# Order of the woven instruction programs written out for the first mixer and the second block's mixers, and chosen anew for the third block

## The chip, the cores and the metric

The kernel runs on one core of one Trainium2 chip. The metric is the device time of one execution in microseconds (us). The engines of the core take their own instruction streams and wait for one another through semaphores: TensorE (PE) multiplies matrices, VectorE (DVE) and ScalarE (ACT) do the elementwise work, GpSimd (POOL) issues gathers, SyncE (SP) issues nearly all other transfers. Everything is fp32; a large product is made of three fp32r products, each operand being split into a high and a low part.

## The reference, cut to what matters

Three transformer blocks follow one another on x (512 rows, 1024 columns).

```python
def first_block(x, c, ...):
    mod = silu(c) @ w_ada + b_ada               # 6 rows of 1024: shift, scale, gate twice
    h = rms_norm(x, norm1_w) * (1 + scale1) + shift1
    q, k, v, cb, cc, cx, iq, ik, iw = split(h @ w_in)
    # indexer: relu(iq . ik) weighted by iw over 8 heads, 128 keys kept for each query
    score = einsum(relu(einsum(iq, ik)), iw); sel = top_k(causal(score), 128)
    y_attn = softmax(rms_norm(q) . rms_norm(k)[sel]) @ v[sel]      # 8 heads of 64
    y_conv = cb * causal_conv3(cc * cx)
    x = x + gate1 * (concat(rms_norm(y_attn), rms_norm(y_conv)) @ w_out)
    return x + gate2 * peer_ffn(rms_norm(x) * (1 + scale2) + shift2, ...)

def second_block(x, ...):
    # band attention (8 heads), gated delta rule (4 heads, chunks of 64, after a conv of 4),
    # four causal window means (pool), three gated branch products, output product
    x = layer_norm(alpha * x + hybrid_mixer(x, ...))
    return layer_norm(alpha * x + hierarchical_moe(x, ...))

def third_block(x, ...):
    # four attentions (forgetting, block-sparse, stick-breaking, sliding window), gates, output product
    return x + concat(o_fox, o_moba, o_sb, o_swa) * silu(gates) @ w_out
```

## The kernel before, in words

The blocks run one after another, each as one or more stages. The first block is `first_mixer` (0 to 468 us of the span; names begin with firsts_) and the retrieval of `peer_ffn` (names peer_). The second is `mixers` (1822 to 2523), the routing and the experts (names slotted_). The third is `third_block` (3180 to 3622, names third_). Rows are kept in four tiles of 128, the contraction of 1024 in eight steps k.

Within `first_mixer`, `mixers` and `third_block` the work of one engine is given as several generator programs. Each yields before a part of its work; what it yields is a number, its estimated due time. `weave` (L1520) merges the programs of one engine: the one with the lowest number goes next. `weave_by` (L1536) merges them by a table instead: "b8 c6" means eight parts of the second program and six of the third. Before the change only the third block uses a table, `THIRD_ORDER`. The order decides in which sequence an engine's instructions stand in its queue; each engine takes its queue in that sequence, and waits where a semaphore isn't there yet.

The programs of `first_mixer`. `loads` (SP) brings c, the first third of w_ada (8 loads of 1 MB, firsts_ada_first), x, the constants; `weights_in` (SP) the pieces of w_in into three buffers firsts_raw; `ada_in` the rest of w_ada. `ada_tensor` multiplies silu(c) with the first four column blocks of w_ada (L649, 64 matmuls), `ada_vector` sums the other eight on DVE (L679, L682, 64 steps), each closed by a matmul L660. `rows_*` make h and its transpose hT (high and low). `rounded` (ACT L801) and `rests` (DVE L809) split a weight piece into high and low; `products` (PE L849) multiplies a piece: 8 steps k of 3 matmuls, 30 pieces, 720 matmuls. `rel_*` are the indexer's scores: PE L997, relu on ACT L1007, weighted sum on DVE L1019 and L1022, closed by L1026; then the picking, 16 rounds of MAX8 (L1033) and MATCH_REPLACE8 (L1038) on DVE. `soft_*` are 32 softmax works n (8 heads by 4 row tiles t, 128(t+1) keys): score L1078 on PE, bias L1119, maximum L1122 and its negation L1123 on DVE, exponential L1101 on ACT, transposes L1082 on PE, copy L1105 on ACT, mix with v L1088 on PE, copy L1126 on DVE (semaphore scaled). Work n uses bank n%2 of two. `closed_*` are the output product (L834 first half, L864 second half) and the second norm.

The programs of `mixers`: `products` (L1774, three matmuls a step k), `rounded` and `rests` (L1788, L1795), `band_*` (score L2050, transposes L2055, mix L2060), `pool_*` (window sums on DVE L1955 to L1958, matmul L1973), `conv_*` (L2252 to L2292), and `delta_*` in two streams for the gated delta rule: its PE steps L2329 to L2388, the norm of its output (square sums L2545, root ACT L2438, L2552, scaling L2555), transposes L2394 and the multiplication with the gate mixers_dg (L2566). The gate goes out to DRAM and comes back; ACT L1838 works on it once it has landed.

In the third block `stick_*` are the stick-breaking works (scores L3985, DVE L4037 to L4049, ACT L4021, PE L3991 and L3998).

## Time and profile before

| | before |
|---|---|
| median of three runs, us | 3620.53 (3618.37 to 3625.39) |
| profiled execution, us | 3623.54 |
| its span, us | 3621.8 |
| mean granted clock of PE, share of full | 0.931 |
| PE busy | 3155.4 us, 87% of the span |
| DVE busy | 2412.2 us, 67% |
| ACT busy | 1399.1 us, 39% |
| first mixer, us | 468 |
| mixers, us | 701 |
| third block, us | 442 |
| one split of a weight piece on DVE (L809), mean | 1.19 us |
| one ada step on DVE (L682), mean | 0.75 us |

In the rows further down a line is an instruction or a group of them: engine, source line, operation, output and inputs by their names, and in square brackets the time that the engine stood idle ahead of it and what ended that. PE matmuls overlap: the distance of two starts tells the rate, the duration doesn't. PEclk is the share of full clock that the throttle granted to PE (0.50 is 1.2 GHz, 1.00 is 2.4 GHz).

### The profile page before, as it was taken

Reading aid. Unit: us, or ns where it says so; the run is one execution under the profiler, and the core shown is the slowest. Engines: PE = TensorE matmul, PEld = TensorE weight load, DVE = VectorE, ACT = ScalarE, POOL = GpSimd, SP = SyncE. Lnnn points to the kernel's source line nnn. Section 1 sums busy time; section 2 is a strip of 40 time slices with the busy share of each in tenths; the row PEclk is TensorE's granted clock in tenths of the full one; section 3 lists DMA queues with packets and bytes.
Section 4 is the critical chain, followed back from the end, with each engine's and each line's share of the span. In section 5 each row is a group of like instructions: output and inputs, shape, how many; then the busy total and the mean of one; then the engine's idle time right before and its main releaser. Section 6 shows DMA issues by size and latency. Waiting matters only on the chain. (4 is left out here: it accounts for less than half of the span.)

```text
span 3621.8 us, 34663 instructions
## 1 busy us (share of the span) xinstructions
PE 3155.4 (87%) x11816; PEld 2012.9 (56%) x11816; DVE 2412.2 (67%) x4718; ACT 1399.1 (39%) x2337; POOL 717.6 (20%) x583
## 2 busy tenths in 40 slices
PE   8988889988787787777788999997599999949998
PEld 4655644433333333333366787776488888836666
DVE  4866446677767776777658445554688888845565
ACT  2323322222222222222243233342488888733564
POOL 0000024344444444444400000000122222100000
PEclk9988899998999899999899999998699999969999
DMA  8322169999999999999942222232799999831111
GB/s 283 111 82 87 47 244 393 404 400 422 421 408 421 417 414 421 413 414 413 416 116 58 65 73 70 68 111 76 257 354 374 377 371 372 317 107 48 53 41 65
DMA packets 351923, 905.62 MB, mean 250 GB/s; under 512 B 29953, under 2 KB 170753, under 8 KB 285570
## 3 DMA queue, kind: packets, MB, share of 16 engines
q0 software_dynamic: 84000, 549.52, 37.1%
q1 hardware_dynamic: 267746, 353.85, 29.0%
q8 instruction: 98, 1.61, 0.2%
q14 instruction: 79, 0.65, 0.1%
HBM read 896.45 MB, written 31.99 MB: 256 GB/s over the span
## 5 line engine op out<-in xcount | busy, mean ns | idle before, releaser
L258 PE MATMUL peer_acc<-peer_uv,peer_diag 128*128 128x512 f32 x2048 | 1004.1, 643 | 228.9 <-ACT peer_diag L314 223.2
L435 DVE CUSTOM_DVE_ANT_0 peer_uv<-peer_uv,firsts_h 128x1024 f32<-128x1024 f32 x512 | 627.3, 1226 | 345.9 <-DMA peer_uv<-in_peer_uv,peer_experts 344.6
L258 PEld LDWEIGHTS peer_acc<-peer_uv,peer_diag 128*128 128x128 f32 x2048 | 410.5, 205 | 803.6 <-issue 494.4
L210 POOL DMA_INDIRECT peer_uv<-in_peer_uv,peer_experts x512 | 593.4, 1159 | 1212.2 <-PE peer_acc L258 692.4
L3066 DVE TENSOR_TENSOR slotted_low<-slotted_raw,slotted_high 128x2048 fp32r<-128x2048 f32 x192 | 434.2, 2289 | 66.6 <-ACT slotted_high L3015 66.6
L3015 ACT ACTIVATE slotted_high<-slotted_raw 128x2048 fp32r<-128x2048 f32 x192 | 365.5, 1920 | 64.4 <-PE slotted_h L2972 51.8
L314 ACT ACTIVATE peer_diag<-all_consts,peer_weights 128x128 f32<-128x128 f32 x512 | 166.1, 391 | 325.6 <-DVE peer_weights L428 300.7
L305 ACT ACTIVATE peer_act_in<-peer_act_in 128x4 f32<-128x4 f32 (+1 forms) x130 | 26.6, 205 | 615.5 <-DVE peer_act_in L435 615.3
L2972 PE MATMUL slotted_h<-slotted_high,slotted_xT_high 128*128 128x512 f32 x512 | 205.2, 401 | 6.2 <-DVE slotted_low L3066 4.1
L2972 PE MATMUL slotted_h<-slotted_high,slotted_xT_low 128*128 128x512 f32 x512 | 201.8, 394 | 0.0
L2972 PE MATMUL slotted_h<-slotted_low,slotted_xT_high 128*128 128x512 f32 x512 | 201.7, 394 | 0.0
L1774 PE MATMUL mixers_acc<-mixers_xT_high,mixers_high 128*128 128x512 f32 x448 | 197.5, 441 | 1.7 <-DVE mixers_low L1795 1.7
L1774 PE MATMUL mixers_acc<-mixers_xT_high,mixers_low 128*128 128x512 f32 x448 | 179.7, 401 | 0.0
L1774 PE MATMUL mixers_acc<-mixers_xT_low,mixers_high 128*128 128x512 f32 x448 | 179.5, 401 | 0.0
L1795 DVE TENSOR_TENSOR mixers_low<-mixers_raw,mixers_high 128x1024 fp32r<-128x1024 f32 (+1 forms) x77 | 93.2, 1210 | 123.9 <-ACT mixers_high L1788 123.4
L2839 POOL MEMSET slotted_xg<- 128x4096 f32 x1 | 3.5, 3511 | 731.4 <-POOLq L60 731.4
L2934 POOL DMA_INDIRECT results<-slotted_ob,slotted_rows_out x32 | 32.3, 1008 | 461.7 <-ACT slotted_ob L3042 447.8
L2972 PEld LDWEIGHTS slotted_h<-slotted_high,slotted_xT_high 128*128 128x128 f32 x512 | 97.5, 190 | 27.3 <-DVE slotted_low L3066 4.3
L2972 PEld LDWEIGHTS slotted_h<-slotted_high,slotted_xT_low 128*128 128x128 f32 x512 | 97.4, 190 | 21.5
L3544 PE MATMUL third_acc<-third_hT_high,third_high 128*128 128x512 f32 x240 | 107.2, 447 | 1.5 <-DVE third_hT_low L3408 1.5
L2972 PEld LDWEIGHTS slotted_h<-slotted_low,slotted_xT_high 128*128 128x128 f32 x512 | 97.6, 191 | 19.2
L849 PE MATMUL firsts_acc<-firsts_hT_high,firsts_high 128*128 128x512 f32 (+1 forms) x240 | 104.7, 436 | 2.9 <-DVE firsts_low L809 2.9
(752 smaller groups left out, 5689.3 us busy)
## 6 DMA issues: line engine op xcount, KB each, us to landing
slotted_raw<-in_moe_w SPq DMA_DIRECT2D x192, 1024.0 KB, 8.1
mixers_raw<-in_w_in SPq DMA_DIRECT2D x56, 512.0 KB, 3.9
firsts_ada_raw<-in_w_ada SPq DMA_DIRECT2D x64, 256.0 KB, 2.8
third_raw<-in_w_in SPq DMA_DIRECT2D x30, 512.0 KB, 3.8
firsts_raw<-in_w_in SPq DMA_DIRECT2D x28, 512.0 KB, 4.2
firsts_ada_first<-in_w_ada SPq DMA_DIRECT2D x8, 1024.0 KB, 13.3
peer_uv<-in_peer_uv,peer_experts POOLq DMA_INDIRECT x512, 10.9
ffn_w_raw<-in_peer_wq SPq DMA_DIRECT2D x10, 512.0 KB, 18.9
```

What stands on the lines that cost most here:

```text
L210: pool.indirect_dma_start(uv[:, n % R, :, :].rearrange("p a d -> p (a d)"), None, A["peer_uv"], bass.IndirectOffsetOnAxis(ap=experts[:, si ...
L258: mm = nc.tensor.matmul(acc[t % 2][j][:, :], diag[:, n % 4, :], uv[:, n % R, 1, j * BANK:(j + 1) * BANK], start=(m == 0), stop=(m == E - 1))
L314: nc.scalar.activation(diag[:, n % 4, :], C["ident"], ACT.Copy, scale=weights[:, side, i:i + 1])\
L435: nc.vector.tensor_tensor_reduce(uv[:, n % R, 0, :], uv[:, n % R, 0, :], h2[:, t, :], 1.0, 0.0, ALU.mult, ALU.add, act_in[:, side, i:i + 1 ...
L849: mm = nc.tensor.matmul(bank[rows, :], b, a, start=(k == 0 and r == 0), stop=(k == KD - 1 and r == 2))
L1774: mm = nc.tensor.matmul(bank[:, :], b, a, start=(k == 0 and r == 0), stop=(k == piece["kb"] - 1 and r == 2))
L1795: nc.vector.tensor_tensor(low[:, p % 2, 0:size], raw[:, p % RAW, 0:size], high[:, p % 2, 0:size].bitcast(F32), ALU.subtract).then_inc(low_ ...
L2934: pool.indirect_dma_start(results, bass.IndirectOffsetOnAxis(ap=rows_out[:, e:e + 1], axis=0), ob[:, e % 2, :], None, bounds_check=2 * L - ...
L2972: mm = nc.tensor.matmul(ps_h[i // 2][:, :], a, b, start=(k == 0 and r == 0), stop=(k == KD - 1 and r == 2))
L3015: nc.scalar.activation(high[:, p % RING, :], raw[:, p % RAW, :], ACT.Copy).then_inc(high_done, 1)
L3066: nc.vector.tensor_tensor(low[:, p % RING, :], raw[:, p % RAW, :], high[:, p % RING, :].bitcast(F32), ALU.subtract).then_inc(low_done, 1)
L3544: mm = nc.tensor.matmul(bank[:, :], b, a, start=(k == 0 and r == 0), stop=(k == KD - 1 and r == 2))
```

## The change

No instruction is added or removed but for table loads of ACT, which follow from the order; the retrieval, the routing and the experts are untouched. What changes:

- `first_mixer` and `mixers` merge by tables too, `FIRST_ORDER` and `MIXERS_ORDER`, for all of SP, PE, ACT and DVE. `THIRD_ORDER` has new contents.
- The programs yield more often, so that a table can part them more finely: `products` after each step k (3 matmuls; before at k = 4 only), the output products likewise, and DVE's chains of small steps (short convolution, pool sums, convolution of four, delta rule) between single steps or small groups.
- In `soft_*` and `band_*` the numbers by which the parts of the works are sorted grow by 2.9 a work (before by `work_key`, mostly 4.0), so that score(n+1) stands ahead of transposes(n).
- The memset of u waits for rows_normed.

```diff
             for n in range(n_works):
-                later += [(work_key[n], 0, n), (work_key[n] + 3.0, 1, n), (work_key[n] + 5.0, 2, n)]
+                at = 2.9 * n
+                later += [(at, 0, n), (at + 3.0, 1, n), (at + 5.0, 2, n)]
...
                 for k in range(KD):
-                    if k == 4:
-                        yield (starts[p] + ends[p]) / 2
+                    if k:
+                        yield starts[p] + (ends[p] - starts[p]) * k / KD
...
                     dve.wait_ge(small_in, 80)
+                    dve.wait_ge(rows_normed, NT)
                     chain(nc.vector.memset(u[:, :, 0:2], 0.0))
...
             @block.tensor
             def _(pe):
-                weave(ada_tensor(pe), rows_tensor(pe), products(pe), spare_tensor(pe), rel_tensor(pe), soft_tensor(pe),
+                weave_by(FIRST_ORDER["tensor"], ada_tensor(pe), rows_tensor(pe), products(pe), spare_tensor(pe), rel_tensor(pe), soft_tensor(pe),
                       closed_tensor(pe))
...
                 for j in range(i + 1):
                     sh, dst = WINDOWS[j] // 2, wsum[:, j % 2, :]
+                    if j:
+                        yield pool_at + 5.0 * i
                     chain(nc.vector.tensor_tensor(dst[:, PADW:], src[:, PADW:], src[:, PADW - sh:PADW + L - sh], ALU.add))
...
+FIRST_ORDER = {
+    "sync": (
+        "b3 a c2 a b2 c2 a c7 b c3 b c3 b c2 b c4 b c3 b c6 b c2 b10 c b c b2 c b c2 b c2 b c b c3 b c2 b c3 b c2 "
```

Three places show what moves. First, the queue of SP at the start of the first block, before:

```order
L607 DMA firsts_c_col<-in_c_col 128x8
L610 DMA firsts_ada_first<-in_w_ada 128x4x512
L613 DMA firsts_norm_row<-in_norm_w 128x1024
L614 DMA firsts_mod_71<-in_b_ada 128x2048
...
L610 DMA firsts_ada_first<-in_w_ada 128x4x512 x3
L618 DMA all_consts<-in_consts 128x3829
L772 DMA firsts_raw<-in_w_in 128x8x128 x3
```

and after:

```order
L772 DMA firsts_raw<-in_w_in 128x8x128 x3
L607 DMA firsts_c_col<-in_c_col 128x8
L610 DMA firsts_ada_first<-in_w_ada 128x4x512
L613 DMA firsts_norm_row<-in_norm_w 128x1024
L614 DMA firsts_mod_71<-in_b_ada 128x2048
```

The three loads of w_in pieces went from behind the constants to the head of the queue. Second, PE where the softmax works go from the third row tile (384 keys) to the fourth (512 keys), before; firsts_mid are the two banks, firsts_qkT the queries and keys:

```order
L1078 MATMUL firsts_mid<-firsts_qkT 128x384
L1088 MATMUL firsts_mid<-firsts_probs,firsts_v_tm 64x128 x3
L660 MATMUL firsts_side<-firsts_acc_last,all_consts 128x512
L1082 MATMUL firsts_mid<-all_consts,firsts_probs 128x128 x3
L1078 MATMUL firsts_mid<-firsts_qkT 128x512
L1088 MATMUL firsts_mid<-firsts_probs,firsts_v_tm 64x128 x3
L1082 MATMUL firsts_mid<-all_consts,firsts_probs 128x128 x4
L1078 MATMUL firsts_mid<-firsts_qkT 128x512
```

and after, where L1083, L1087, L1093 and L851 are the lines L1078, L1082, L1088 and L849 of before:

```order
L1083 MATMUL firsts_mid<-firsts_qkT 128x384
L1087 MATMUL firsts_mid<-all_consts,firsts_probs 128x128 x3
L851 MATMUL firsts_acc<-firsts_hT_high,firsts_high 128x512
L851 MATMUL firsts_acc<-firsts_hT_high,firsts_low 128x512
L851 MATMUL firsts_acc<-firsts_hT_low,firsts_high 128x512
L1093 MATMUL firsts_mid<-firsts_probs,firsts_v_tm 64x128 x3
L851 MATMUL firsts_acc<-firsts_hT_high,firsts_high 128x512
L851 MATMUL firsts_acc<-firsts_hT_high,firsts_low 128x512
L851 MATMUL firsts_acc<-firsts_hT_low,firsts_high 128x512
L1083 MATMUL firsts_mid<-firsts_qkT 128x512
L1087 MATMUL firsts_mid<-all_consts,firsts_probs 128x128 x3
```

Three products now stand behind the transposes and three behind the mix, and the score of the next work ahead of the transposes. Third, ACT at the end of the mixers, before; mixers_dg is the gate of the delta rule, mixers_osum the square sums under its root:

```order
L2433 ACTIVATE mixers_o<-mixers_delta 64x256 x2
L1788 ACTIVATE mixers_high<-mixers_raw 128x1024
L1838 ACT_TABLE_LOAD
L1838 ACTIVATE mixers_dg<-mixers_dg 128x2048
L1852 ACT_TABLE_LOAD
L1852 ACTIVATE mixers_gate_11773<-mixers_gate_11773,mixers_gb 128x512 x4
L1831 ACTIVATE mixers_gate_11773<-mixers_acc 128x512
L1788 ACTIVATE mixers_high<-mixers_raw 128x1024
L2438 ACT_TABLE_LOAD
L2438 ACTIVATE mixers_osum<-mixers_osum 128x4x2 x2
```

and after (L2451, L1796, L2456, L1846 and L1839 are L2433, L1788, L2438, L1838 and L1831 of before):

```order
L2451 ACTIVATE mixers_o<-mixers_delta 64x256 x4
L1796 ACTIVATE mixers_high<-mixers_raw 128x1024 x2
L2456 ACT_TABLE_LOAD
L2456 ACTIVATE mixers_osum<-mixers_osum 128x4x2
L1796 ACTIVATE mixers_high<-mixers_raw 128x1024
L2456 ACTIVATE mixers_osum<-mixers_osum 128x4x2
L1796 ACTIVATE mixers_high<-mixers_raw 128x1024
L1846 ACT_TABLE_LOAD
L1846 ACTIVATE mixers_dg<-mixers_dg 128x2048
L1839 ACTIVATE mixers_gate_11774<-mixers_acc 128x512 x2
```

The root went ahead of the gate's activation, which waits for a transfer.

## Rows read from the trace of the kernel before

**Rows 1.** Page, busy time of each engine over the whole span.
```profile
PE 3155.4 (87%) x11816; PEld 2012.9 (56%) x11816; DVE 2412.2 (67%) x4718; ACT 1399.1 (39%) x2337; POOL 717.6 (20%) x583
```

**Rows 2.** Timeline of PE: start, duration, engine, line, operation; products at low clock.
```profile
284.19 0.63 PE L849 MATMUL firsts_acc<-firsts_hT_high,firsts_low 128*128 128x512 f32 x1
284.62 0.63 PE L849 MATMUL firsts_acc<-firsts_hT_low,firsts_high 128*128 128x512 f32 x1
```

**Rows 3.** Timeline of PE, mixers: products, one small step between, at full clock.
```profile
2062.28 0.39 PE L1774 MATMUL mixers_acc<-mixers_oT_high,mixers_low 128*128 128x512 f32 x1
2062.51 0.39 PE L1774 MATMUL mixers_acc<-mixers_oT_low,mixers_high 128*128 128x512 f32 x1
2062.83 0.65 PE L2378 MATMUL mixers_delta<-mixers_S,mixers_wT 128*64 128x128 f32 x4
2063.41 0.50 PE L1774 MATMUL mixers_acc<-mixers_oT_high,mixers_high 128*128 128x512 f32 x1
2063.75 0.40 PE L1774 MATMUL mixers_acc<-mixers_oT_high,mixers_low 128*128 128x512 f32 x1
```

**Rows 4.** Windows of the first mixer: busy by engine, PEclk, DMA share, GB/s.
```profile
0.00:40.00 40.00, 31.49 (x64) 12.60 (x64) 8.48 (x11) 7.67 (x12) 0.20 (x4) 1.00 0.97 363
224.00:334.00 110.00, 100.26 (x435) 68.98 (x434) 73.65 (x152) 37.09 (x84) 0.00 (x0) 0.92 0.36 108
334.00:412.00 78.00, 63.19 (x237) 38.85 (x235) 38.94 (x79) 29.93 (x60) 0.00 (x0) 0.73 0.10 31
412.00:468.00 56.00, 43.63 (x201) 35.92 (x202) 32.19 (x46) 19.24 (x39) 0.00 (x0) 0.87 0.18 57
```

**Rows 5.** Windows of the mixers, same columns: PE, PEld, DVE, ACT, POOL.
```profile
1880.00:2020.00 140.00, 116.77 (x465) 87.52 (x464) 105.13 (x142) 55.41 (x79) 0.00 (x0) 0.89 0.21 57
2200.00:2240.00 40.00, 35.79 (x198) 28.19 (x197) 27.40 (x82) 14.22 (x37) 0.00 (x0) 0.96 0.21 65
```

**Rows 6.** Windows of the third block, same columns.
```profile
3380.00:3560.00 180.00, 176.89 (x853) 113.19 (x851) 109.69 (x263) 108.47 (x227) 0.00 (x0) 0.99 0.16 43
3560.00:3580.00 20.00, 13.13 (x90) 10.99 (x90) 16.40 (x32) 13.22 (x18) 0.00 (x0) 0.83 0.16 54
```

**Rows 7.** Timeline of PE, one period of two softmax works of 512 keys.
```profile
388.07 0.60 PE L1082 MATMUL firsts_mid<-all_consts,firsts_probs 128*128 128x128 f32 x4
388.60 1.12 PE L1078 MATMUL firsts_mid<-firsts_qkT 64*128 64x512 f32 x2
...
389.65 1.09 PE L1088 MATMUL firsts_mid<-firsts_probs,firsts_v_tm 128*64 128x128 f32 x8
...
392.26 0.66 PE L1082 MATMUL firsts_mid<-all_consts,firsts_probs 128*128 128x128 f32 x4 [1.52 <-ACT firsts_probs L1101]
```

**Rows 8.** Timeline of PE, the first product of the first mixer.
```profile
52.91 0.77 PE L849 MATMUL firsts_acc<-firsts_hT_high,firsts_high 128*128 128x512 f32 x1 [2.89 <-DVE firsts_low L809]
```

**Rows 9.** Timeline: last sum of the indexer, first picking round, first head's score.
```profile
134.33 0.69 DVE L1026 SCALAR_TENSOR_TENSOR firsts_sel<-firsts_sel,all_consts 128x512 f32<-128x512 f32 x1
...
137.41 1.48 DVE L1033 MAX8 firsts_best<-firsts_sel 128x8 f32<-128x256 f32 x3
...
224.34 0.48 PE L1078 MATMUL firsts_mid<-firsts_qkT 64*128 64x128 f32 x2
```

**Rows 10.** Timeline of PE, mixers: waits for a pool sum and for band attention.
```profile
2003.98 2.08 PE L1973 MATMUL mixers_mid<-mixers_u,mixers_pw 128*128 128x512 f32 x2 [4.21 <-DVE mixers_u L1958]
...
2211.76 0.44 PE L2055 MATMUL mixers_mid<-all_consts,mixers_probs 128*128 128x128 f32 x2 [1.75 <-ACT mixers_probs L2087]
```

**Rows 11.** Timeline, end of the mixers' delta rule.
```profile
2436.20 1.91 ACT L1838 ACTIVATE mixers_dg<-mixers_dg 128x2048 f32<-128x2048 f32 x1 [7.24 <-DMA mixers_dg<-gates_home]
...
2446.82 1.11 PE L2394 MATMUL mixers_delta<-all_consts,mixers_o 128*128 128x128 f32 x4 [9.45 <-DVE mixers_o L2555]
...
2455.64 0.77 PE L1774 MATMUL mixers_acc<-mixers_oT_high,mixers_high 128*128 128x512 f32 x1 [4.42 <-DVE mixers_oT_low L2570]
```

**Rows 12.** Timeline of PE, third block, inside the second window.
```profile
3568.63 1.97 PE L3991 MATMUL third_stick<-all_consts,third_lg 128*128 128x128 f32 x8 [6.34 <-DVE third_lg L4049]
```

More of the change, by code:

```diff
@@ L827, in products @@
                     for t in range(NT):
-                        if kp < 2:
-                            pe.wait_ge(y_low, 4 * t + 4)
                         for kk in range(2):
+                            if t or kk:
+                                yield starts[p] + (ends[p] - starts[p]) * (2 * t + kk) / KD
+                            if kp < 2 and kk == 0:
+                                pe.wait_ge(y_low, 4 * t + 4)
                             k = 2 * kp + kk
@@ L1094, in soft_scalar @@
             for n in range(n_works):
-                later += [(work_key[n] + 2.0, 0, n), (work_key[n] + 4.0, 1, n)]
+                at = 2.9 * n
+                later += [(at + 2.0, 0, n), (at + 4.0, 1, n)]
             for key, what, n in sorted(later):
@@ L1110, in soft_vector @@
             for n in range(n_works):
-                later += [(work_key[n] + 1.0, 0, n), (work_key[n] + 6.0, 1, n)]
+                at = 2.9 * n
+                later += [(at + 1.0, 0, n), (at + 6.0, 1, n)]
             for key, what, n in sorted(later):
@@ L1396, in _ @@
             def _(sp_queue):
-                weave(loads(sp_queue), weights_in(sp_queue), ada_in(sp_queue))
+                weave_by(FIRST_ORDER["sync"], loads(sp_queue), weights_in(sp_queue), ada_in(sp_queue))
                 sp_queue.wait_ge(gate2_out, 16)
@@ L1761, in products @@
                         for k in range(piece["kb"]):
-                            if k and k % 2 == 0 and (name, m) in lent:
-                                yield starts[p] + LENT_PIECE * k / KD
-                            elif k == 4:
-                                yield starts[p] + HALF
+                            if k:
+                                yield starts[p] + (ends[p] - starts[p]) * (i / 2 + k / KD)
+                            if k == 4:
                                 if p == 1:
@@ L2080, in band_scalar @@
             for n in range(n_works):
-                later += [(work_key(n) + 2.0, 0, n), (work_key(n) + 4.0, 1, n)]
+                later += [(step_key(n) + 2.0, 0, n), (step_key(n) + 4.0, 1, n)]
             for key, what, n in sorted(later):
@@ L2500, in delta_vector @@
                 chain.join()
+                yield hop(s, t, 10)
                 for h in heads:
@@ L2575, in _ @@
             def _(sp):
[L2576 removed]
+                weave_by(MIXERS_ORDER["sync"], weights_in(sp), small_loads(sp), lending(sp), returning(sp))
             @block.tensor
             def _(pe):
[L2580 removed]
+                weave_by(MIXERS_ORDER["tensor"], turn_tensor(pe), products(pe), pool_tensor(pe), band_tensor(pe), decay_tensor(pe), conv_tensor(pe),
                       delta_tensor(pe, 0), delta_tensor(pe, 1))
```

55 lines of the change are left out of this document (43 added, 12 removed), and 62 rows, old and new, of tables (FIRST_ORDER, MIXERS_ORDER, THIRD_ORDER).

## The prediction

> **What bounds the kernel now.** I read the summary of the page first: the TensorE (PE) is busy 3155 of 3621.8 us [rows 1]. No instruction is added or taken away by the change, so it can only give back time in which PE idles or runs at the lower clock, and only in the stretches whose order is rewritten: first mixer (0 to 468 us), mixers of the second block (1822 to 2523), third block (3180 to 3622). Retrieval and slotted experts keep their time.
>
> Then the windows. For each stretch I work out what PE would need at the full clock, as busy time times granted clock, since products start 0.43 us apart where the clock is at its 1.2 GHz level and 0.227 apart at 2.4 GHz [rows 2, 3]. Late first mixer: 100.3 x 0.92 + 63.2 x 0.73 = 138 of 188 us [rows 4]. Its closing stretch 412 to 468: 43.6 x 0.87 = 38 of 56. Mixers, 1880 to 2020: 116.8 x 0.89 = 104 of 140; 2200 to 2240, the first of two alike: 35.8 x 0.96 = 34.4 of 40 [rows 5]. In most of the rest of these blocks PE is near full, as in 3380 to 3560: 176.9 of 180 at 0.99 [rows 6].
>
> Last, which wait ends those idle times. In the late first mixer PE stands at the transposes of the softmax, L1082, for the exponentials of ACT L1101: in the timeline of two heads 388.07 to 392.26 is one period of 4.19 us, and PE idles 1.52 of it ahead of the next transposes [rows 7]. DVE there is busy 73.7 + 38.9 = 112.6 of 188, so it bounds nothing yet.
>
> **First mixer, start.** The three firsts_raw loads (0.5 MB each) go ahead of the ada weights on SP. PE's first 40 us are a stream of L649 on those weights, with the DMA engines 0.97 busy at 363 GB/s [rows 4]. 1.57 MB / 363 GB/s = 4.3 us that every ada load comes later. Since the first piece is then split early, half of the 2.89 us wait for L809 before the first product goes [rows 8]: -1.4. The ada steps of DVE now placed among the hT_low steps cost one of about 0.7. Net +3.5; ends +1.5 (the loads overlap) and +5.
>
> A rule bears on this. The Trainium skill, "DMA: Bandwidth & Descriptors", section "Queues, rings and completion order", says that on each DMA engine the descriptors of one ring are consumed in ring order. The row agrees so far as these loads share SP's queue and the engines are full. By the rule the whole 4.3 us is paid; with fair sharing it would be about half.
>
> **First mixer, scorer.** The rel steps (L997, L1007, L1022) stand between products 121 and 178, before between 157 and 252. The last one ended at 134.33 us, and the first head's score ran at 224.34 [rows 9]. With 74 fewer products in front (74 x 0.227 = 17 us of PE) less the 3.5 and less what ACT and DVE now have to squeeze in, I take the end at 126. The picking, 16 rounds on DVE from 137.41 on, and the norms keep their length: 224.3 - 137.4 = 87. 126 + 87 = 213: heads start 11 us earlier, the 3.5 included. Ends 0 (if the picking is stretched by the ada steps put between its rounds) and -14.
>
> **First mixer, heads.** Before, the last ten of 32 softmax works had no products left between them; the order was transposes(n), score(n+1), mix(n). Now score(n+1) stands ahead of transposes(n), three products follow, mix(n), three products. All 32 works find cover (products 487 to 720). From the end of the score to the next transposes DVE and ACT need 392.26 - 389.65 = 2.6 us; PE now has transposes 0.53, products 6 x 0.227 = 1.36, mix and score 1.05 each, 4.0 in all: covered [rows 7]. From transposes to mix the rows have 389.65 - 388.60 = 1.05 us; three products fill 0.68, some 0.25 stays open, x 32 = 8. What is added: 38 more changes between products and small steps. One change there and back costs (2062.83 - 2062.51) + (2063.75 - 2063.41) - 2 x 0.227 = 0.2 us [rows 3]: 7.6. What leaves the stretch: 48 products of the output, L834, at 0.227 = 10.9. So 138 - 10.9 + 7.6 = 135, plus 8, plus 9 for waits not seen: 152 against 188, -36. The idle time of PE there now is 24.6, so the waits kept lie between 0 and 24.6. The 48 products join the closing stretch: 38 + 10.9 = 49 of work, with 11 of the present 18 of idle and slow clock kept: 60 against 56, +4. Sum of the heads -32; ends -49 (no waits) and -10.
>
> Start to end that is -43. I hold back 7, as DVE's 112.6 us plus ada steps must now fit in 152 at 74% in an order in which one long step (1.2 us) ahead of a bias add is a wait of PE: **-36**.
>
> **Mixers.** In 1880 to 2020 the long waits are those for DVE's pool sums, three to six steps in one go (4.21 us at 2003.98, three such) [rows 10], and smaller ones for the squares. Each DVE step is now placed singly among products. I take half of the 140 - 104 = 36: -18; ends 0 and -33. In the two stretches of 40 PE waits at band attention (1.75 at 2211.76) [rows 10]: 40 - 34.4 = 5.6 a stretch, 11 in both, -8; ends 0 and -11.
>
> Tail: ACT's queue has the gates' activation L1838 ahead of the root L2438 of the delta rule's norm. L1838 waits for its DMA until 2436.20, so the transposes L2394 run at 2446.82, 9.45 us of idle, and the next product at 2455.64, 4.42 more [rows 11]. After the change the root stands first and the DMA wait lies beside products; the chain left is root, scale, transposes, multiply, split. -11, at most -13.9.
>
> Against it: three places where band or delta steps of both streams now stand with three or fewer products between them; I put twice the band's wait on each, 3 x 3 = +9. Sum **-28**, ends -5 and -45.
>
> **Third block.** One wait of 6.34 us at L3991 stands in a stretch of 20 us with 13.1 x 0.83 = 10.9 of work [rows 6, 12]. The last stick work is started some 100 products earlier, so the wait and the slow clock behind it go: -7. The rest of the block has 180 - 176.9 = 3.1 us of idle in its longest stretch; its new order is worth 0, with 4 either way.
>
> Sum: -36 - 28 - 7 = -71. The profiled execution took 3623.5 (span 3621.8), 3 above the median: 3623.5 - 71 = 3552.5, less 3: **3550**.
>
> **Rivals.** *Cover only in part.* DVE takes its steps in order; with two foreign steps (1.2 for the split of a weight piece, 0.75 for an ada step) ahead of a bias add the chain 2.6 + 1.95 is over the 4.0 of cover, and with the 0.25 above one work costs 0.8 to 1 us. 32 us instead of 17: heads -17 instead of -32, start -4 instead of -11, mixers half (-14), third 0: -35, less 3: 3586. For it: every exponential has three DVE steps ahead of it. Against: DVE's share stays under 75%.
>
> *Nearly all idle recovered.* Heads -49, start -11, mixers -42 (-30, -10, -11, +9), third -7: -109, 3512. For it: 3380 to 3560 is woven work by such an order already, at 0.99.
>
> *The clock stays low, slower than before.* In 334 to 412 the granted clock is 0.73 [rows 4] with idle times of only one to two us between heads. If the weave leaves short waits throughout and the clock sits at the 1.2 GHz level for the 32 heads, the products are spaced 0.43 instead of 0.227 [rows 2, 3], and the 135 us of work become about 250 instead of 152: +98 on the forecast, 3648. It turns to slower than before when some 70% of the stretch is at that level. Against it: in 224 to 334, where heads lie among products, the clock is 0.92. The Trainium skill, "TensorE: Matmul & The Clock Gate", section "A second HAM failure mode: psum-queue depth-cycling", describes this: a TensorE that pauses briefly between groups of matmuls swings between its clocks. The 0.73 agrees with it, the 0.92 doesn't.
>
> *The order differs and the waits don't.* Each wait is met at another place (the exponentials take as long, ACT and DVE are as late): 3617.
>
> **Chances.** Forecast 0.48 (3535 to 3572); in part 0.20 (3575 to 3600); nearly all 0.17 (3500 to 3530); low clock 0.09; no change 0.06. Leaving out the last two and the lowest part of the third gives 3505 to 3605; the ends of the terms, -49 - 14 and -45 in sum, lie under it only all at once. A measurement can tell about 0.2% (7 us) from no change. Faster 0.48 + 0.20 + 0.17 = 0.85, same 0.06, slower 0.09.
>
> **What would show it.** Right: the first score of a head before 216; heads and products ended by about 370 with the granted clock over 0.9; PE's waits for the exponentials under 10 us in sum; first mixer 432 long, mixers 673; the transposes of L2394 waiting under 3 us. Wrong at the start: the ada stream ends at 40 as before. Wrong in the heads: DVE steps between score and bias add, PE's share under 80% there. Wrong in all: mean clock under 0.93.

## The result, and the profile after

The changed kernel takes 3500.52 us (median of 4 runs, 3496.51 to 3505.96) against 3619.53 for the kernel before beside it: ratio 0.9668, 95% interval 0.9654 to 0.9682. That is 119 us or 3.3% faster; the forecast was 71 less, and the time lies 4.5 us under the range. PE's mean granted clock rose from 0.931 to 0.949. The number of PE, DVE and POOL instructions is the same.

Where the time went is read from the timeline of PE, by the first or last matmul of each stage. The middle columns are the two profiled executions, the last one is a second profile of the changed kernel, taken with a later set of runs.

| stretch (by its marks on PE) | before | after | difference | forecast | after again |
|---|---|---|---|---|---|
| first mixer, to the first matmul of the retrieval | 467.9 | 423.3 | -44.6 | -36 | 422.3 |
| retrieval (not changed), to the first matmul of the mixers | 1357.6 | 1364.6 | +7.0 | 0 | 1360.2 |
| mixers, to the first transposes of the routing | 721.6 | 657.5 | -64.1 | -28 | 658.6 |
| routing, experts, start of the third block, to its first transposes | 667.4 | 661.7 | -5.7 | 0 | 663.4 |
| third block, from there to the last matmul | 403.7 | 389.9 | -13.8 | -7 | 389.0 |

The retrieval's code and order are the same; its length was 1356.5 to 1364.6 in the 18 profiles of this case, with the DMA engines at a share of 1.01 before (500 to 1800 us) and 1.00 after (500 to 1780). Its +7 is such a difference between executions. The other stages vary too: with its code as before the first mixer took 463.7 to 467.9 us in three profiles and the mixers 717.3 to 721.6 in three; in their new order the first mixer took 418.8 to 423.3 in nine (and 432.7 in one more, see the last section), the mixers 655.7 to 658.6 in eight. So the first mixer gains 40 to 49 us and the mixers 59 to 66.

The windows of the first mixer, profile after (columns as in rows 4; they answer to the second to fourth row there):

```profile
221.00:353.00 132.00, 129.32 (x611) 78.92 (x612) 99.06 (x206) 57.78 (x126) 0.00 (x0) 1.00 0.33 100
353.00:366.00 13.00, 4.26 (x15) 2.93 (x14) 12.38 (x21) 4.38 (x10) 0.00 (x0) 0.61 0.00 1
366.00:423.00 57.00, 50.65 (x248) 41.38 (x246) 36.23 (x54) 20.44 (x44) 0.00 (x0) 0.95 0.20 65
```

All 32 softmax works now fit into 132 us in which PE is busy 129.3 at full clock. Behind them stands a new hole of 13 us. The timeline of PE, profile after, with the marks of the start, one softmax work of 512 keys among products, and the hole (it answers to rows 7 to 9):

```profile
11.20 1.19 PE L649 MATMUL firsts_side<-firsts_ada_first,firsts_c_col 128*128 128x512 f32 x1 [11.20 <-DMA firsts_ada_first<-in_w_ada]
57.52 0.77 PE L851 MATMUL firsts_acc<-firsts_hT_high,firsts_high 128*128 128x512 f32 x1 [2.47 <-DVE firsts_hT_low L731]
...
340.23 1.09 PE L1093 MATMUL firsts_mid<-firsts_probs,firsts_v_tm 128*64 128x128 f32 x8
341.25 0.50 PE L851 MATMUL firsts_acc<-firsts_hT_high,firsts_high 128*128 128x512 f32 x1
...
342.14 1.12 PE L1083 MATMUL firsts_mid<-firsts_qkT 64*128 64x512 f32 x2
343.19 0.66 PE L1087 MATMUL firsts_mid<-all_consts,firsts_probs 128*128 128x128 f32 x4
343.60 0.47 PE L851 MATMUL firsts_acc<-firsts_hT_high,firsts_high 128*128 128x512 f32 x1
...
344.54 1.09 PE L1093 MATMUL firsts_mid<-firsts_probs,firsts_v_tm 128*64 128x128 f32 x8
...
362.16 2.04 PE L660 MATMUL firsts_side<-firsts_acc_last,all_consts 128*128 128x512 f32 x2 [8.74 <-DVE firsts_acc_last L682]
```

No brackets in the middle: from mix to mix 4.31 us, 0.1 more than rows 7's period, but with six products in it.

The mixers, windows of the profile after, and the tail in PE's timeline (they answer to rows 5 and 11). The long waits of PE of the former kernel are gone, but for a new one in the tail:

```profile
1842.00:1900.00 58.00, 55.60 (x222) 40.84 (x221) 56.95 (x55) 31.89 (x39) 0.00 (x0) 1.00 0.28 74
1900.00:1960.00 60.00, 59.99 (x321) 48.19 (x320) 50.23 (x95) 24.50 (x43) 0.00 (x0) 1.00 0.28 79
```

```profile
1928.70 1.12 PE L1985 MATMUL mixers_mid<-mixers_u,mixers_pw 128*128 128x512 f32 x2
...
2335.59 1.04 PE L2412 MATMUL mixers_delta<-all_consts,mixers_o 128*128 128x128 f32 x8
...
2356.65 0.77 PE L1782 MATMUL mixers_acc<-mixers_oT_high,mixers_high 128*128 128x512 f32 x1 [9.59 <-DVE mixers_oT_low L2596]
```

The waits of PE over the whole of this stage by line (total, times, longest in us), the three largest before and the two largest after, and the stage as one window, before and after:

```profile
PE mixers_mid L1973 <- DVE mixers_u L1958: 11.9, 3, 4.2
PE mixers_delta L2394 <- DVE mixers_o L2555: 9.9, 2, 9.4
PE mixers_delta L2292 <- DVE mixers_sq L2261: 7.8, 5, 3.0
```

```profile
PE mixers_acc L1782 <- DVE mixers_oT_low L2596: 9.6, 1, 9.6
PE mixers_mid L1690 <- PEq L189: 3.2, 1, 3.2
```

```profile
1825.00:2547.00 722.00, 647.89 (x3206) 513.08 (x3206) 407.55 (x807) 260.04 (x459) 5.09 (x3) 0.94 0.28 83
```

```profile
1788.00:2445.00 657.00, 622.93 (x3206) 494.69 (x3205) 407.52 (x803) 260.69 (x458) 5.10 (x3) 0.98 0.30 91
```

The 3.2 us for PEq, PE's own sequencer, are in both kernels.

In the first 118 us of that stretch PE is busy 115.6 at full clock and DVE 107.2. The pool matmul (row at 1928.70) starts without a wait, where rows 10 have 4.21 us. In the third block the wait of rows 12 is gone too: L4017, the line L3991 of before, starts its last 8 at 3448.02 without one.

### The profile page after: what moved, and what is told of

It is laid out like the page before. It is cut to its first block and busy times, and to the rows that moved or that the text cites. A ratio compares the mean times of both kernels' runs of the same rounds, so it can differ in the third digit from the quotient of the medians.

```text
span 3500.5 us, 34680 instructions
## 1 busy us (share of the span) xinstructions
PE 3097.1 (88%) x11816; PEld 1968.4 (56%) x11816; DVE 2415.5 (69%) x4718; ACT 1397.3 (40%) x2332; POOL 705.2 (20%) x583
## 5 line engine op out<-in xcount | busy, mean ns | idle before, releaser
L210 POOL DMA_INDIRECT peer_uv<-in_peer_uv,peer_experts x512 | 580.9, 1135 | 1183.1 <-PE peer_acc L258 708.9
L1782 PE MATMUL mixers_acc<-mixers_xT_high,mixers_high 128*128 128x512 f32 x448 | 189.5, 423 | 1.9 <-DVE mixers_low L1803 1.9
L2865 POOL MEMSET slotted_xg<- 128x4096 f32 x1 | 3.5, 3512 | 671.3 <-POOLq L60 671.3
L1796 ACT ACTIVATE mixers_high<-mixers_raw 128x1024 fp32r<-128x1024 f32 (+1 forms) x77 | 80.4, 1047 | 124.0 <-PE mixers_acc L1782 98.2
```

The costliest lines, as they stand in the source:

```text
L210: pool.indirect_dma_start(uv[:, n % R, :, :].rearrange("p a d -> p (a d)"), None, A["peer_uv"], bass.IndirectOffsetOnAxis(ap=experts[:, si ...
L1782: mm = nc.tensor.matmul(bank[:, :], b, a, start=(k == 0 and r == 0), stop=(k == piece["kb"] - 1 and r == 2))
L1796: nc.scalar.activation(high[:, p % 2, 0:size], raw[:, p % RAW, 0:size], ACT.Copy).then_inc(high_done, 1)
```

## The experiments

The whole question behind them: does such an order give back all that a stage loses, down to PE's work at full clock, because each waiting step stands where its operand is ready? Or only a part, as the prediction has it, since chains of DVE and ACT stay? The letters of the theories in the expectations hold within their own run. Small effects are read by stage from the profiles, since the medians of the same kernel differ: those of the kernel before lie between 3619.3 and 3625.8 us in five sets of runs.

**Each stage alone.** The first function (or table) after, the other two before:

```diff
-first_mixer (after), mixers (after), THIRD_ORDER (after)
+first_mixer (after), mixers (before), THIRD_ORDER (before)     # and the two other choices
```

> Only the first mixer is rewritten, mixers and third block as before. Theory A (each stage's gain is its own, as the two traces have it: first product of the retrieval at 423.3 against 467.9, -44.6): 3575 us, the mixers 701 long. Theory B (the stages' gains hang together, by the clock or the DMA queues, and the first mixer alone is worth what the prediction gave it, -36, or less): 3584 or more.

> Only the mixers are rewritten, first mixer and third block as before. Theory A (own gain, mixers 637 long against 701): -64, 3556 us. Theory B (prediction's size, half of the idle time): -28, 3592 us.

> Only the third block has its new table. Theory A (425.3 long against 445.1): -20, 3600 us. Theory B (only the wait of 6.34 us at the end goes): -7, 3613 us.

| | ratio (interval) | median, us | its own stage in the profile |
|---|---|---|---|
| first mixer alone | 0.9887 (0.986 to 0.9914) | 3578.8 | 418.8 to the retrieval |
| mixers alone | 0.9816 (0.9795 to 0.9837) | 3558.9 | 657.6 |
| third alone | 0.9940 (0.9919 to 0.9961) | 3600.8 | 389.1 |

The kernel before took 3624.2 beside them. By the ratios the parts are worth 41, 67 and 22 us, in sum 130 against the 120 of the whole, and each is uncertain by 8 to 10 us: within the intervals each stage's gain is its own. Theory A holds for the mixers and the third block. For the first mixer alone 3578.8 lies between theory A and theory B, whose times are both inside its interval, and it is the length of the stage, 418.8 against 463.7 to 467.9, that speaks for A. The three terms of the prediction were each too small, those of the mixers and of the third block by more than half.

**Finer yields without the table.**

```diff
-                weave_by(MIXERS_ORDER["tensor"], turn_tensor(pe), products(pe), ...
+                weave(turn_tensor(pe), products(pe), ...            # and the three other engines
...
-            return work_at + 2.9 * n
+            return work_at + TAU * n
```

> The changed kernel, but the mixers' programs, with all their finer yields, are merged by the estimated due times again, not by the table. Theory A (the places that the table gives the small steps bring the gain): the mixers lose half or more of their 64 us, 3532 us or more. Theory C (the finer yields alone bring it, any sensible merge will do): within 10 us of the changed kernel, 3500 to 3510.

3574.7 us (ratio 0.9861, 0.984 to 0.9882): theory A. The mixers are 731.6 long, 10 to 14 more than before the change. PE's waits in the mixers, its longest three by line:

```profile
PE mixers_mid L1985 <- DVE mixers_u L1970: 12.4, 3, 5.3
PE mixers_delta L2310 <- DVE mixers_sq L2278: 10.1, 5, 4.6
PE mixers_delta L2412 <- DVE mixers_o L2581: 9.7, 2, 9.3
```

The old waits are back, each of the three about as long in sum as before the change, or longer. Merged by these due times the finer parts are worth nothing; the gain is in the places that the table gives them.

**DVE's chains.** In the table of DVE the steps of each window sum follow at once on the first:

```diff
 L1965 TENSOR_TENSOR mixers_wsum<-mixers_u 128x512
-L1965 TENSOR_TENSOR mixers_wsum<-mixers_wsum 128x512
+L1965 TENSOR_TENSOR mixers_wsum<-mixers_wsum 128x512 x2
+L1968 TENSOR_TENSOR mixers_wsum<-mixers_wsum,mixers_inv 128x512
+L1970 TENSOR_TENSOR mixers_u<-mixers_wsum,mixers_u 128x512
```

> The changed kernel, but DVE takes the three to six steps of each window sum in one go again (8 of 18 steps move). Theory A (the prediction's: splitting DVE's chains gives back the waits of PE in this stretch): the mixers lose 5 to 12 us, 3508 us. Theory B (where PE's waiting step stands among the products decides, not where DVE's chain is cut): within 2 us of 637 for the mixers, 3500 us.

3502.8 us, mixers 659.0 against 655.7 to 658.6 in the eight profiles with the changed order. Theory B: cutting the pool sums apart on DVE, which the prediction named as the reason of that term, brings no more than 3 us, hardly told from nothing.

**PE's waiting step.** Two pool matmuls go ahead by 18 and 9 products (letters c and b of PE's table), all else stays. What the expectation leaves out: the first of them also goes ahead of 32 records of small matmuls of the delta rule (L2347 to L2356), so that it comes 8.1 us of PE's work earlier, not 4.1.

> The changed kernel with two of the four pool matmuls on PE (L1985) moved ahead, one by 18 products, one by 9, DVE's order untouched; with products 0.227 us apart they are reached 4.1 and 2.0 us earlier, and stand 0.9 and 0 us behind DVE's last step now. Theory A (the place of PE's waiting step is what the table set right in this stretch, and the idle time goes 1:1 into the stage, with up to half as much again at the lower clock): two waits of 5 us in sum, mixers 5 to 8 us longer, 3506 us. Theory B (other engines catch up behind a wait, so that it is mostly given back): 0 to 2 us.

3520.0 us (0.972, 0.9694 to 0.9745), with 3503.0 for the changed kernel beside it; mixers 671.1, 12.5 longer than in the profile beside it and 12.5 to 15.4 longer than in all eight. PE's timeline of this run, then DVE's last step of the sum that the first of them needs; behind these the same two steps in the changed kernel:

```profile
1908.36 2.08 PE L1985 MATMUL mixers_mid<-mixers_u,mixers_pw 128*128 128x512 f32 x2 [7.05 <-DVE mixers_u L1970]
...
1933.38 1.26 PE L1985 MATMUL mixers_mid<-mixers_u,mixers_pw 128*128 128x512 f32 x2 [2.05 <-DVE mixers_u L1970]
```

```profile
1907.61 0.69 DVE L1970 TENSOR_TENSOR mixers_u<-mixers_wsum,mixers_u 128x512 f32<-128x512 f32 x1
```

```profile
1912.80 0.69 DVE L1970 TENSOR_TENSOR mixers_u<-mixers_wsum,mixers_u 128x512 f32<-128x512 f32 x1
1914.44 1.02 PE L1985 MATMUL mixers_mid<-mixers_u,mixers_pw 128*128 128x512 f32 x2
```

Theory A, and stronger than expected. In the changed kernel the step starts 0.95 us behind DVE's last one; moved ahead of 8.1 us of PE's work it is 7.2 short, and waits 7.05. So a wait of 9.1 us in sum costs 12.5, a third more. The rest is clock: in the 8 us from the first of them on the granted clock was 0.64, behind the second 0.79:

```profile
1908.00:1916.00 8.00, 7.46 (x23) 5.10 (x24) 0.30 (x1) 1.81 (x4) 0.00 (x0) 0.64 0.00 0
1933.00:1941.00 8.00, 7.62 (x33) 5.93 (x33) 6.21 (x16) 1.34 (x3) 0.00 (x0) 0.79 0.14 29
```

While PE stands, the other engines run dry: DVE's next step behind the row above starts at 1919.32, after 11.0 us of idle.

**Is DVE a bound there?**

```diff
+                    chain(nc.vector.tensor_tensor(dst[:, PADW:], src[:, PADW:], src[:, PADW - sh:PADW + L - sh], ALU.add))
                     chain(nc.vector.tensor_tensor(dst[:, PADW:], src[:, PADW:], src[:, PADW - sh:PADW + L - sh], ALU.add))
```

> The changed kernel with each of the ten additions of the window sums done twice on DVE (same operands, same result), 7.0 us of DVE work in the mixers' first 120 us, where DVE is busy 107 of 118 us. Theory A (in that stretch PE and DVE are now bound together, which is why half of its idle time was too little to expect and all of it came): mixers 4 to 8 us longer. Theory B (PE alone bounds it and DVE has room): 0 to 1 us.

Mixers 661.3, 2.7 more than in the profile beside it and 2.7 to 5.6 more than in all eight, for 7.0 us of added work: between the two theories, nearer to A. The same window in this run, and in the changed kernel beside it:

```profile
1842.00:1960.00 118.00, 111.92 (x528) 86.12 (x526) 108.87 (x156) 50.66 (x76) 0.00 (x0) 1.00 0.28 76
```

```profile
1842.00:1960.00 118.00, 115.99 (x554) 90.19 (x553) 105.40 (x148) 53.97 (x81) 0.00 (x0) 1.00 0.28 76
```

PE loses 4.1 us of busy time as DVE gains 3.5. The stretch is near the limit of both engines; the earlier kernel had 35 us of DVE's time free in its 140 (rows 5), and 36 of PE's with its work taken at full clock.

**What covers the softmax chain.** Two changes of the changed kernel: transposes(n) ahead of score(n+1) again,

```diff
-                at = 2.9 * n
+                at = 3.1 * n
```

> The changed kernel, but in the first mixer transposes(n) stand ahead of score(n+1) again, all products where they are. Theory A (the score ahead of the transposes gives the softmax chain its cover: without it 2.6 us of PE work lie over a chain of 2.6 us plus whatever DVE does in between): waits for the exponentials of 0.5 to 1 us a work, +15 to +30 us, 3515 to 3530. Theory B (products between the works are cover enough): 3500 to 3505 us.

and, in PE's table, the three products between transposes(n) and mix(n) moved behind the mix at 21 works:

```diff
-f2 c f c
+f3 c2
```

> The changed kernel with the three products between transposes(n) and mix(n) moved behind mix(n), at 21 works of the first mixer. Theory A (PE has 1.05 us of its own from transposes to mix, and what isn't covered is idle): about 1 us each, less 0.2 for the change of kind saved: +17, 3517 us, with waits of L1093 for L1111. Theory C (what costs is the number of changes between products and small steps): -4, 3496 us.

From the first score to the last mix the changed kernel takes 131.4 us (131.4 to 131.5 in every profile that has this order there). Transposes first: 138.5, +7.1; median 3502.5 us. Without cover before the mix: 145.6, +14.2; median 3509.0 us (0.9687, 0.9663 to 0.9711). The waits of PE for the exponentials and the copies of the transposes, in the first run and then in the second:

```profile
PE firsts_mid L1087 <- ACT firsts_probs L1107: 2.4, 3, 1.8
...
PE firsts_mid L1093 <- ACT firsts_probs L1111: 0.7, 1, 0.7
```

```profile
PE firsts_mid L1093 <- ACT firsts_probs L1111: 11.4, 22, 0.7
```

So theory A of the first was right in sign and much too large (+7 instead of +15 to +30). Its own timeline says where the 7 are: 3.9 of them are lost ahead of the first mix already. There the first transposes stand right behind the first score and wait, and behind that wait the granted clock was 0.50 until about 222:

```profile
219.11 0.48 PE L1087 MATMUL firsts_mid<-all_consts,firsts_probs 128*128 128x128 f32 x1 [1.84 <-ACT firsts_probs L1107]
...
317.17 0.60 PE L1087 MATMUL firsts_mid<-all_consts,firsts_probs 128*128 128x128 f32 x4
...
321.47 0.60 PE L1087 MATMUL firsts_mid<-all_consts,firsts_probs 128*128 128x128 f32 x4
```

From there to the last mix 3.2 us are added over 31 works, and the last two rows, one work of 512 keys apart, are 4.30 us apart, as in the changed kernel. So between works theory B nearly holds: with products on both sides the place of the score is worth 0.1 us a work. Theory A of the second was nearly right in size: 0.5 us a work where nothing lies between transposes and mix, and some 2 us of slow clock (0.50 at 340 us) on top. In the changed kernel, with three products there, that line has one wait of 0.7 us, at the last work, behind whose transposes no products are left. The 0.25 a work that the prediction left open did not exist.

**The start.** Weight loads behind the ada weights again, the first roundings and rests with them:

```diff
-"b3 a c2 a b2 c2 a ..."      # SP: b weight pieces, a other loads, c ada weights
+"a b3 c2 a b2 c2 a ..."
-"b2 a9 b c b ..."            # ACT: b roundings
+"a9 b3 c b ..."
-"a c2 a4 b2 a b a b7 d ..."  # DVE: c rests, a ada steps
+"a5 b2 a b a b7 c2 d ..."
```

> The changed kernel with the first three loads of w_in pieces, their roundings on ACT and two rests on DVE put back behind the ada weights, x and constants. Theory A (the queue is served in order and the loads are bound by the DMA engines, so 1.5 MB ahead cost 4.2 us): first ada matmul at 7.0 instead of 11.2, first product at 53.5 instead of 57.5, 3496.5 us. Theory B (the early pieces pay for themselves by products that don't wait at the start): no gain, 3500 us or more.

3505.2 us. The first ada matmul came at 6.63, 4.6 earlier, and the first product at 65.74, 8.2 later:

```profile
56.09 0.38 SPq L772 DMA_DIRECT2D firsts_raw<-in_w_in  x1
57.23 0.38 SPq L772 DMA_DIRECT2D firsts_raw<-in_w_ik  x1
57.65 1.27 SPq L635 DMA_DIRECT2D firsts_ada_raw<-in_w_ada  x2
```

```profile
65.74 0.76 PE L851 MATMUL firsts_acc<-firsts_hT_high,firsts_high 128*128 128x512 f32 x1 [12.52 <-DVE firsts_hT_low L731]
```

Theory A was right on the queue and wrong on the rest, and by the time theory B holds, for another reason than its own: the first mixer is 429.4 long, 6 us more. The fourth weight load on SP waits for the first rest on DVE; with the rests late it was issued at 56.09 instead of 41.84, and the ada loads stood behind it, issued from 57.65 on. These loads landed 2.6 to 5.3 us after their issue, and DVE idled 5.8 us up to an ada step at 62.98, ahead of the last hT_low. The early rests clear SP's queue. Loads, roundings and rests were moved together, so what the loads alone do was not tried.

**The hole behind the works.** DVE takes the last ada step ahead of the convolution's reciprocal, its add behind the norm steps, PE's L1233 two steps later:

```diff
-a3 d g d8 a e2 a e5      # DVE
+a4 d g d8 a e7
-a d c7 d c2              # PE
+a c2 d c5 d c2
```

> The changed kernel, the last ada step of the first mixer on DVE ahead of the convolution's reciprocal (3.35 us) and norm steps, its closing add right behind them, and PE's L1233 two steps later. The changed kernel has a wait of 8.7 us at L660 there. Theory A (that step and its add hold the output product): output product 3.5 us earlier, 3497 us. Theory B (the convolution's chain, done at 361.3, holds it as well): 0 to 1.5 us.

L660 waits 0.57 us now, and the output product 8.46 for the last low part of the convolution:

```profile
351.17 1.10 PE L660 MATMUL firsts_side<-firsts_acc_last,all_consts 128*128 128x512 f32 x2 [0.57 <-DVE firsts_acc_last L682]
360.73 0.77 PE L836 MATMUL firsts_side<-firsts_high,firsts_yT_high 128*128 128x512 f32 x1 [8.46 <-DVE firsts_yT_low L959]
```

It starts 11.2 us behind the last mix instead of 13.2, and the retrieval 72.0 instead of 70.9: nothing gained in the end, theory B. (The median is 3497.4, and no more below those of the changed kernel, 3500.5 and 3503.0, than medians of one kernel differ.)

**Start of the third block.** Two weight splits back in their old place:

```diff
-"a13 b a3 b a4 c b ..."   # ACT: a row steps, b roundings
+"a3 b2 a17 c b ..."
```

> The changed kernel with the first two weight splits of the third block back in their old place on ACT and DVE (behind the third row tile's sums, ahead of the norms). Theory A (they wait for their loads and hold the norm chain behind them: ACT idles 5.6 us for the load in the kernel before): first transposes of the third block 5 to 6 us later, 3506 us. Theory B (the norm chain's own length sets the start): 3500 us.

From the last expert matmul to the first transposes 42.2 us against 35.0 to 37.2 in the 14 other profiles with the new third block, and 41.4 to 42.1 in three with the old one; whole 3508.4 us. ACT in this run:

```profile
3096.93 1.06 ACT L3514 ACTIVATE third_high<-third_raw 128x1024 fp32r<-128x1024 f32 x1 [6.06 <-DMA third_raw<-in_w_in]
```

Theory A: the norm chain's squares stood behind a rounding that waits for its load. The new table takes the rounding later.

**The tail of the mixers.** First the two last loads of gates swapped on SP:

```diff
             yield gate1_at
-            wait_multiplied(sp, "o0", KD - 1)
-            ...
-            sp.dma_start(gate[1][:, 0:LENT, :], ...).then_inc(gate1_back, 16)
-            yield dg_at
             wait_emptied(sp, "o0", KD - 1)
             sp.dma_start(dg[:, :, :], ...).then_inc(dg_back, 16)
+            yield dg_at
+            ...
+            sp.dma_start(gate[1][:, 0:LENT, :], ...).then_inc(gate1_back, 16)
```

> The changed kernel with the two last loads of lent gates swapped on SP: mixers_dg (1 MB) ahead of mixers_gate (1.5 MB). In the changed kernel PE waits 9.6 us ahead of the first product of oT for a chain that starts when mixers_dg has landed, 8.7 us after its issue. Theory A (that landing holds the tail): it lands about 4 us earlier, the mixers are 3 to 4 us shorter, 3497 us. Theory B (another step of ACT or DVE in the same place holds it): no change, 3500 us.

3500.4 us, the same wait: theory B. mixers_dg landed 5.7 us after its issue instead of 8.7, and nothing came of it:

```profile
2347.37 1.29 DVE L1892 TENSOR_SCALAR mixers_dg<-mixers_dg,mixers_gain 128x2048 f32<-128x2048 f32 x1 [4.28 <-ACT mixers_dg L1846]
2351.46 0.60 ACT L1839 ACTIVATE mixers_gate<-mixers_acc 128x512 f32<-128x512 f32 x1 [3.50 <-PE mixers_acc L1782]
2351.95 1.99 ACT L1796 ACTIVATE mixers_high<-mixers_raw 128x1024 fp32r<-128x1024 f32 x2
2353.03 2.36 DVE L1803 TENSOR_TENSOR mixers_low<-mixers_raw,mixers_high 128x1024 fp32r<-128x1024 f32 x2 [4.38 <-ACT mixers_high L1796]
2355.30 2.48 DVE L2592 TENSOR_TENSOR mixers_dv<-mixers_delta,mixers_dg 128x512 f32<-128x512 f32 x4
```

Read upwards: the multiplication L2592 has its gate at 2348.7 and stands behind two rests, these behind ACT's rounding, this behind the emptying of a bank that PE fills last. So, on top of the swap:

```diff
-c b2 k2 j2 k2 j2 c d      # DVE: b rests, k and j the two delta streams
+c b k2 j2 k2 j2 b c d
-c2 b2 d k2 j2 d e         # ACT: c banks emptied, b roundings
+c b k2 j2 c b d2 e
```

> The run with mixers_dg loaded first, and in addition the gate multiplications and splits of the delta rule's output (L2592, L2461, L2596) placed ahead of ACT's emptying of the last product bank (L1839) and DVE's second rest (L1803). Theory A (the tail is held by in-order queues: DVE's multiply stood behind two rests, these behind ACT's rounding, that behind a bank that PE fills last): PE's wait of 9.6 us ahead of the first oT product falls to 2 to 3, the mixers are 6 to 7 us shorter, 3494 us. Theory B (another chain of the same length stands behind): the wait stays over 7.

3492.1 us (0.9652, 0.9626 to 0.9678), mixers 649.6, 6 to 9 shorter, PE's wait 3.4:

```profile
2344.49 0.76 PE L1782 MATMUL mixers_acc<-mixers_oT_high,mixers_high 128*128 128x512 f32 x1 [3.40 <-DVE mixers_oT_low L2596]
```

Theory A. Together with only two of the first three weight loads ahead:

```diff
-"b3 a c2 a b2 ..."
+"b2 a b c2 a b2 ..."
```

> The kernel with the unblocked tail of the mixers, and only two of the three first weight loads ahead of the ada weights. Theory A (gains of stages add up, and the third early load only delays): first ada matmul 1.4 us earlier, 3491 us, 9 to 10 us under the changed kernel of the same call. Theory B (the third load is needed early as well): no gain over the unblocked tail alone, 3492 to 3494 us.

> The changed kernel once more on the chip of this call, as a measure for the others: 3500 us, within 5 us.

3494.3 us (5 runs) against 3503.0 for the changed kernel beside it, 8.7 less. The first ada matmul came at 9.55, the first product at 58.67 instead of 57.78: the load order gives nothing (theory B), the tail gives all of it. In single runs the two kernels overlap (3488.3 to 3506.4 and 3497.9 to 3508.3); the stage in the profiles does not (651.0 and 649.6 against 655.7 to 658.6).

## Why the prediction was right or wrong, point by point

Of the 50 us by which the forecast was short in the profiled executions, 36 are the mixers, 13 the third block with its start, 9 the first mixer; the retrieval took back 7. The steps that failed are named below, each in the words of the prediction: half of the idle time of the mixers kept, 17 us for waits in the heads, a new order of the third block "worth 0".

**What bounds the kernel, and the additivity of stages: right.** Only the three stages moved beyond what executions differ by, and their gains add up. PE's work at full clock was worked out as 138 us for the late first mixer; the same product over the whole first mixer, busy time times granted clock, gives 361 us before (405.4 x 0.89) and 362 after (376.7 x 0.96). So the order hardly changes it. In the heads the new order gets there, 132 us for 129 of work; over the whole first mixer it doesn't, 423 us for 362, with the start and the closing stretch still full of waits.

**Start of the first mixer: right.** +3.5 forecast, +4.6 measured (first product 52.91 to 57.52), the ada stream 4.2 later for 1.5 MB ahead of it in the queue. By the Trainium skill's rule of ring order in "DMA: Bandwidth & Descriptors", section "Queues, rings and completion order", it was to be the whole 4.3: the row agrees. The wait of 2.89 us for L809, half of which was to go, is gone, but PE waits 2.47 for the last hT_low in its place. What the early steps are good for, a free queue for the ada loads behind them, was not seen.

**Scorer: direction right, size wrong.** The last indexer sum stood at 128.8 instead of the forecast 126 (134.3 before), and from the first picking round to the first score it took 91 us instead of 87, with ada steps between the rounds: -3.4 instead of -11 (-3.6 to -7.6 in most other profiles). The first score came at 221.0, not before 216.

**Heads: mechanism right, waits put in that aren't there.** The step that failed is "plus 8, plus 9 for waits not seen". The bound of 135 was worked out from rows; measured are 131.4 from the first score to the last mix, where the forecast had 152. It is the products between that do it, as the runs without one of the two show: +14 without the products ahead of the mix, though the score kept its place, and +7 with the transposes first, more than half of it at the first work. The 7 us held back for DVE were wrong as well: PE waited 1.5 us for DVE's copies and norms in the heads.

**Closing stretch: wrong.** +4 forecast, 58.2 to 70.9 measured, from the last mix on. The 10.9 us of moved products were right; the step that failed is "with 11 of the present 18 of idle and slow clock kept", since 22 are there now. The hole of 8.7 at L660 was in the order to be read: the last ada step on DVE stands behind the convolution's reciprocal. The run that moved it shows the convolution's chain of nearly the same length behind it.

**Mixers: the main miss, -28 against -64.** "I take half of the 36" had no row behind it. In the windows of after the first 118 us of the stretch have 2.4 us of idle. The reason given, DVE steps singly among products, was wrong: the pool sums in one go cost 0.4 to 3.3 us. It is the place of the steps that wait, PE's above all; two of them put 8.1 and 2.3 us of PE's work ahead cost 12.5 us, and the old merge with the fine parts brings the waits back. "+9 for thin places" was wrong: PE has no wait there. The waits for band attention, forecast at -8, are gone as forecast (L2050 and L2055, 7.8 us in sum before). Over the whole stage PE's idle time fell from 74 to 34 us, and the stage by 64: the other 25 are PE's busy time, 648 to 623 us at a mean clock of 0.94 and 0.98, the clock that comes back when waits go, as in the run with the two early steps. Some 5 of these 25 are not the change's: with the mixers unchanged PE was busy for 642 to 643 us in two other profiles. The tail was forecast at -11 and gave 4.3 (9.45 + 4.42 against 9.59), since the wait was passed on to a queue of DVE and ACT, for which no row was looked up. In 1825 to 1880 the clock of 0.88 rose to 0.97, but that is no gain of the order: the first 55 us of the unchanged mixers had 0.97 in both other profiles of them.

**Third block: -7 against -19.5.** The wait at the end went, as forecast. The step that failed is "its new order is worth 0". Two gains were not looked for. One is 5.7 us at the start, where ACT stood for a load ahead of the norm chain, shown by the run that puts it back. The other is in the block itself, 13.8 us shorter: PE's idle time fell by 9 us, of which 6.3 are the wait that was forecast, and its busy time by 5, 384.8 to 379.6 at a clock of 0.96 and 0.97. No run parts these, and two other profiles of the unchanged block are 2.5 shorter and 2.8 longer.

**Rivals.** "Nearly all idle recovered" at 3512 was the one that came, with a chance of 0.17. Its sum is partly luck: its mixers (-42) and third block (-7) were still too small, and the start of the heads and the closing stretch came out worse than it had them. "Cover only in part" fails on DVE's steps hardly ever being late in the heads (1.5 us in sum), "the order differs and the waits don't" on the waits that are gone. The clock rival fails: in 221 to 353, with the most changes between kinds of matmul, the granted clock is 1.00. The Trainium skill's "TensorE: Matmul & The Clock Gate", section "A second HAM failure mode: psum-queue depth-cycling", tells of swings of the clock where TensorE pauses briefly between groups of matmuls. It did not apply, as hardly any pause was left between the groups: 2.7 of 132 us.

## What to carry to other kernels

PE's busy time multiplied by the granted clock over a stage is a floor that hardly moves when only the order does. When a change places every step of every engine anew, forecast that floor plus the holes that remain, and look for those by name, in the new order: where no product is left to cover, and where a step stands behind one that waits on its own queue. A step that waits in an in-order queue is worth moving later rather than cutting finer: one of them, placed ahead of 8.1 us of PE's work with 0.95 to spare, waited 7.05, and the whole loss was a third larger than the waits. Count all that a step passes when it is moved, small steps too. Moving a load or a step alone often only passes the wait to the next step in that queue, as three of these runs show.

## What the runs showed of the hardware

The same instructions of the first mixer, after the same waits, ran at another granted clock in one of the profiles. First the run with the first mixer alone, then that with the swapped gate loads:

```profile
100.00:120.00 20.00, 18.92 (x61) 9.02 (x62) 16.13 (x30) 7.95 (x17) 0.00 (x0) 1.00 0.37 105
120.00:140.00 20.00, 18.89 (x76) 12.39 (x76) 18.49 (x36) 8.85 (x15) 0.00 (x0) 1.00 0.31 86
```

```profile
100.00:120.00 20.00, 18.59 (x36) 8.30 (x36) 13.51 (x25) 5.62 (x13) 0.00 (x0) 0.55 0.27 79
120.00:140.00 20.00, 19.70 (x52) 9.31 (x52) 10.60 (x15) 6.96 (x12) 0.00 (x0) 0.77 0.30 92
```

The first score came at 216.91 in the one and at 230.63 in the other. In both PE had waited 1.6 us for L682, until 100.61 and 100.94. Of the 15 profiles with the new first mixer or a variant of it, eleven have 1.00 in the first of these windows, three 0.91 and this one 0.55. So at this place the clock can go either way in the same order, and that is worth more than most of the single edits tried here: this first mixer is 432.7 long, the others of the same order 418.8 to 423.3. Why it falls in one execution and not in the other stays open.
